# The store of each expert block's result moves from ScalarE's DMA queue to GpSimd's, behind a later gather

## The reference, cut to what matters

```python
def expert_block(args):
    e, tok, g = args
    xb = ht[tok]
    hid = jax.nn.silu(xb @ w1[e]) * (xb @ w3[e])
    return (hid @ w2[e]) * g[:, None].astype(ht.dtype)

yb = lax.map(expert_block, (blk_e, slot_tok.reshape(n_blocks, MOE_BLOCK), slot_gate.reshape(n_blocks, MOE_BLOCK)))
out = jnp.zeros_like(ht).at[slot_tok].add(yb.reshape(n_slots, -1))
```

## Time and profile before

| | us |
|---|---|
| median of 3 runs | 1793.36 |
| lowest and highest run | 1793.09, 1797.89 |
| span of the profiled execution | 1795.6 |
| PE busy in it | 1488.8 (83%) |
| DVE busy | 1117.0 (62%) |
| ACT busy | 684.6 (38%) |
| POOL busy | 239.6 (13%) |
| MoE blocks of layer 0, first gather to last store landed | 509.2 to 941.6 |
| MoE blocks of layer 1, first gather to last store issued | 1409.1 to 1758.5 |

### The profile page before, as it was taken

One profiled execution on the slowest core, in us unless ns is written; L12 is line 12 of the kernel. 1 busy time (PEld: TensorE's weight loads), 2 busy tenths in 40 slices (PEclk: granted clock), 3 DMA queues, 4 the chain that ended last, 5 costly groups with the idle time before them and its releaser, 6 DMA issues. The chain is left out here.

```text
span 1795.6 us, 21028 instructions
## 1 busy us (share of the span) xinstructions
PE 1488.8 (83%) x6626; PEld 1046.2 (58%) x6627; DVE 1117.0 (62%) x1421; ACT 684.6 (38%) x807; POOL 239.6 (13%) x172
## 2 busy tenths in 40 slices
PE   3889997579559999999972998999996499999981
PEld 2444554234248778778862444787743477777871
DVE  2289999853568764866517123655634688887744
ACT  3201010121137754755425002333311377777732
POOL 0000000000011110201102001555500010211201
PEclk9999998789769999999995997999998699999995
DMA  9465764020079977995828002000010799999964
GB/s 316 138 214 187 249 223 170 3 82 36 24 258 374 388 258 262 389 350 188 303 82 304 20 0 94 2 1 1 1 49 34 257 340 382 390 377 383 374 232 176
DMA packets 154127, 354.93 MB, mean 198 GB/s; under 512 B 6128, under 2 KB 23264, under 8 KB 154080
## 3 DMA queue, kind: packets, MB, share of 16 engines
q1 hardware_dynamic: 137552, 298.68, 45.5%
q0 software_dynamic: 8784, 31.99, 5.0%
q10 hardware_dynamic: 7744, 23.68, 3.3%
HBM read 318.57 MB, written 35.75 MB: 197 GB/s over the span
## 5 line engine op out<-in xcount | busy, mean ns | idle before, releaser
L1344 DVE TENSOR_TENSOR W_LO<-WRAW,W_HI 128x2048 fp32r<-128x2048 f32 x192 | 430.9, 2287 | 166.9 <-ACT W_HI L1268 166.8
L1268 ACT ACTIVATE W_HI<-WRAW 128x2048 fp32r<-128x2048 f32 x192 | 356.8, 1908 | 190.6 <-DMA WRAW<-in_moe_w 152.6
L1205 PE MATMUL PS<-W_HI,XLO 128*128 128x512 f32 x624 | 254.7, 408 | 34.7 <-DVE XLO L1353 34.7
L1207 PE MATMUL PS<-W_HI,XHI 128*128 128x512 f32 x624 | 249.0, 399 | 0.0
L1206 PE MATMUL PS<-W_LO,XHI 128*128 128x512 f32 x624 | 248.2, 398 | 0.0
L970 PE MATMUL PS<-HT,RING 128*128 128x512 f32 (+1 forms) x512 | 173.0, 494 | 6.8 <-DVEq L1041 6.8
L1205 PEld LDWEIGHTS PS<-W_HI,XLO 128*128 128x128 f32 x624 | 120.6, 193 | 67.4 <-issue 38.1
L970 PEld LDWEIGHTS PS<-HT,RING 128*128 128x128 f32 x512 | 96.5, 192 | 85.8 <-issue 72.4
L1744 POOL TENSOR_SCALAR HT<-HT,AR 128x512 f32<-128x512 f32 (+1 forms) x64 | 110.2, 1723 | 235.9 <-DVE AR L1699 235.6
L1207 PEld LDWEIGHTS PS<-W_HI,XHI 128*128 128x128 f32 x624 | 120.1, 192 | 26.4
L1205 PE MATMUL PS<-W_HI,HLO 128*128 128x512 f32 x312 | 126.5, 405 | 10.7 <-DVE HLO L1365 9.5
(11 more groups left out here) (220 smaller groups left out, 1971.6 us busy)
## 6 DMA issues: line engine op xcount, KB each, us to landing
WRAW<-in_moe_w SPq DMA_DIRECT2D x96, 2048.0 KB, 12.0
RING<-in_w_mod SPq DMA_DIRECT2D x24, 2048.0 KB, 14.3
moe_out<-YO ACTq DMA_DIRECT2D x39, 512.0 KB, 7.1
RING<-in_conv_pw SPq DMA_DIRECT2D x16, 512.0 KB, 5.3
moe_out<-NIL SPq DMA_DIRECT2D x15, 512.0 KB, 13.3
ROWS<-rows_of_layer SPq DMA_DIRECT2D x12, 512.0 KB, 5.9
RING<-in_attn_w_qkv SPq DMA_DIRECT2D x3, 2048.0 KB, 15.8
moe_in<-RING SPq DMA_DIRECT2D x10, 512.0 KB, 2.6
```

What stands on the lines that cost most here:

```text
L1205: pe.matmul(to, lo, W_HI[:, q, at:at + 512], start=start, stop=False)
L1207: return pe.matmul(to, hi, W_HI[:, q, at:at + 512], start=False, stop=stop)
L1268: nc.scalar.activation(part(W_HI, q, p), part(WRAW, q, p), ACT.Copy).then_inc((w2_hi if q == 2 else w_hi)[L], 1)
L1344: nc.vector.tensor_tensor(part(W_LO, q, p), part(WRAW, q, p), part(W_HI, q, p).bitcast(F32), ALU.subtract).then_inc(lo[L], 1)
```

## The change

ACT keeps the copy to `YO` but no longer issues the store. POOL issues it: after the gather of block b has been issued, POOL waits for `ya_ready` to reach b-1 (ACT's copy of block b-2), issues the store of block b-2, and goes on to wait for the gather of block b+1. The semaphore `y_out`, which counts stores landed, is no longer shared by the two layers but one for each. Nothing else changes: the same 39 stores of 512 KB are made.

```diff
-        y_out = both("y_out")
+        y_out = [sem(f"y_out{L}") for L in range(2)]
@@ gpsimd
-                    with pool.Fori(1, n + 1) as b:
+                    def gather_next(b):
                         pool.wait_ge(xg_in[L], b * 16)
                         pool.wait_ge(xg_turned[L], b)
                         pool.wait_ge(idx_ready[L], 1)
@@
                         gather()
+
+                    def y_store(count, rows):
+
+                        pool.wait_ge(ya_ready[L], count)
+                        pool.dma_start(yd[L][rows, :], YO[:, :]).then_inc(y_out[L], 16)
+
+                    gather_next(1)
+                    gather_next(2)
+                    y_store(1, slice(0, P))
+                    with pool.Fori(3, n + 1) as b:
+                        gather_next(b)
+                        y_store(b - 1, bass.ds(b * P - 2 * P, P))
+                    y_store(n, bass.ds(n * P - P, P))
                     pool.wait_ge(xg_in[L], n * 16 + 16)
@@ scalar
-                    def y_store(b, rows):
+                    def y_copy(b):
                         act.wait_ge(w2_used[L], b + 1)
                         if not first(b):
                             act.wait_ge(y_out[L], b * 16)
                         nc.scalar.activation(YO[:, :].rearrange("p (a n) -> p a n", a=2), PS[:, 5:7, :],
                                              ACT.Copy).then_inc(ya_ready[L], 1)
-                        act.wait_ge(ya_ready[L], b + 1)
-                        act.dma_start(yd[L][rows, :], YO[:, :]).then_inc(y_out[L], 16)
```

More of the change, by code:

```diff
@@ L1309, in _, with block_step @@
                     silu(0)
-                    def block_step(b, rows):
+                    def block_step(b):
                         before, load = load_of(act, b - 1), load_of(act, b)
@@ L1315, in block_step @@
                         split_new(b, before, load, 1)
-                        if rows is not None:
-                            y_store(b - 2, rows)
+                        if not (isinstance(b, int) and b == 1):
+                            y_copy(b - 2)
                             split_new(b - 1, load_of(act, b - 2), before, 2)
@@ L1322, in block_step @@
                         hid_hi(b - 1)
-                    block_step(1, None)
-                    block_step(2, slice(0, P))
+                    block_step(1)
+                    block_step(2)
                     with act.Fori(3, n) as b:
-                        block_step(b, bass.ds(b * P - 2 * P, P))
+                        block_step(b)
                     last = last_block(act)
-                    y_store(act.value_load(INFO[0:1, LAST_BUT_ONE:LAST_BUT_ONE + 1], min_val=least - 2, max_val=nb - 2),
-                            bass.ds(last * P - P, P))
+                    y_copy(act.value_load(INFO[0:1, LAST_BUT_ONE:LAST_BUT_ONE + 1], min_val=least - 2, max_val=nb - 2))
                     split_new(last, load_of(act, last - 1), load_of(act, last), 2)
                     hid_hi(last)
-                    y_store(last, bass.ds(last * P, P))
+                    y_copy(last)
                 @block.vector
```

## The result

| | kernel before | changed kernel |
|---|---|---|
| median (us) | 1795.62 (1793.09 to 1799.93, 4 runs) | 1816.90 (1813.57 to 1828.57, 4 runs) |
| ratio | 1 | 1.0116, 95% interval 1.0078 to 1.0154 |
| span of the profiled execution (us) | 1795.6 | 1811.4 |

The change makes the kernel slower by 1.2%, some 21 us; 1858 was predicted, +64.6. In a second, larger set of runs it stood at 1813.31 us, ratio 1.0076 (1.0051 to 1.01). Direction and mechanism were right, the size was not: it is a third of the forecast. The profiled executions lie 15.8 us apart.

The account below looks back on a forecast made before the run. PE was nearly full, the DMA engines too where weights are new; the change would make a closed loop through the late gather set the pace. Layer 0 +27.2, layer 1 +34.8, ends +2.6: +64.6, so 1858 us, range 1797 to 1905.

Parts of the forecast that it names:

- The heavy loop: Turn to turn where w3 of one block and w2 of the block before are new: 20.7 us before the clock.
- the store on POOL: POOL's issue of the store within the heavy loop: 1.6 us, between ends of 0.94 and 2.99.
- `icur` copy: POOL's copy between store and gather in the heavy loop: 0.6 us, between 0.18 and 2.22.
- landing: From the gather's start to its landing in a heavy step: 9.6 us, between 9.1 and 11.3.
- clock, mean per heavy step: PE's waits lower the granted clock in every second heavy step, at 1.9 us a drop: 0.9 us per heavy step.
- the ends: The end of each layer: last store lands 1.8 us later, ACT's relief gives -0.5; together +2.6 us for both layers.
- Light steps: Steps in which w3 of one block and w2 of the block before aren't both new: 18.1 us, between 17.7 and 18.8.
- ACT's relief: ACT loses 0.53 us of issue per block: worth nothing in the loop, -0.5 us before each layer's last `HHI`.
- the gather still lands in time: Rival, chance 0.18: with the lower ends the loops keep the pace of the kernel before, 1796 us.
- Faster: Rival, chance 0.06 for over 0.3%: ACT's relief brings w2 loads forward 0.5 us and removes PE's waits, at most to 1772.
- Much slower: Rival, chance 0.12: the gather's rows wait in POOL's queue behind the store's, 2.5 us in 35 steps, 1944 us.
- DMA share: Sign in heavy steps: the DMA engines' share falls to about 0.85 to 0.9 as PE waits.

Follow-up runs that it names:

- the first experiment: The changed kernel with each store still on POOL but moved one gather later, gather of block b before the store of block b-3: 1797.77 us, ratio 0.9987.
- the seventh experiment: The changed kernel, with ACT again waiting for its own `YO` copy before going on, though it issues no store: 1787.99 us, ratio 0.9941.
- the longer chain: The changed kernel with nine small POOL copies and a wait for them between the store and the next gather: 1984.19 us, ratio 1.1017.
- the sixth experiment: The changed kernel with the same wait for the `YO` copy, but behind it first the gather, then the store, both on POOL: 1804.51 us, ratio 1.003.

## Why the prediction was right, and where it wasn't

**The mechanism held.** Store soon after the `YO` copy, gather about 9 us behind the turn (10 was said), PE waiting for `XG` and no longer for `XLO`: as said. The heavy loop was put at 20.7 us and is 19.54 in the step above:

| term | predicted | measured |
|---|---|---|
| turn's end to the end of `YO` | 6.6 | 6.62 |
| to the store's start | 0.19 | 0.69 |
| the store on POOL | 1.6 | 0.56 |
| gap | 0.3 | 0 |
| `icur` copy | 0.6 | 0.21 |
| to the gather's start | 0.75 | 0.76 |
| landing | 9.6 | 9.6 |
| the turn | 1.04 | 1.10 |
| clock, mean per heavy step | 0.9 | about 0.1 |

**The step that failed** is the size of two terms of the heavy step, 21.6 us forecast and 19.6 measured: POOL's instructions between copy and gather, and the clock. First POOL. For the store, between 0.94 and 2.99, I took 1.6, and it takes 0.56, below both ends. The Trainium skill (SBUF — State Buffer, Who interferes with whom) says that DVE with two SBUF inputs holds up those instructions of GpSimd that read SBUF, and infers that descriptor writing, which needs the other interface, isn't held up by it. The trace agrees for the plain store: 0.57 us in the median of 39 stores, even inside a `W_LO` group (1623.91 in the first experiment). The `icur` copy was overrated by 0.4, for another reason: it falls between two groups of DVE (`W_LO` ends at 1529.17 and begins again at 1530.23). The gap of 0.3 isn't there. Together these three were 1.7 us too much; 0.5 us too little for the store's start leave 1.2 per heavy step. (Why POOL starts the store 0.69 us behind the copy, where ACT needed 0.19, isn't shown.) The clock, 0.9 forecast and 0.1 measured, makes the other 0.8.

**A right term by luck.** The landing, 9.6, was read from ten gathers of which seven are held up by DVE (2.24 to 3.08 us on POOL), and it came out right because the changed kernel holds up nearly every one (2.74). The seventh experiment has the same order of store and gather with a free gather, and that lands after 7.1 us. The prediction has no term for this.

**The clock.** I charged every second heavy step with 1.9 us. In the two loops of the changed kernel there are two drops, both in layer 1, of 3.4 us each. The first comes right behind a wait of PE, and the stretches are (columns as in the earlier trace rows):

```profile
1657.30:1659.30 2.00, 0.00 (x0) 0.00 (x0) 2.00 (x2) 0.00 (x0) 0.00 (x0) 1.00 1.04 412
1659.50:1662.90 3.40, 3.40 (x13) 3.01 (x13) 1.69 (x3) 1.69 (x2) 0.00 (x0) 0.50 1.03 416
```

The second also follows a wait, of 1.92 us; PE's other waits for `XG`, up to 2.3 us, were followed by none. A drop costs less here than in the earlier trace rows, too: the two steps are 20.57 and 20.85 us long against about 19.6, so 1.0 to 1.3, and PE's next wait is shorter for it (1.06 and 1.29). The kernel before has three drops in the same loop, the changed one two, so the change didn't add to them; I had charged for the new ones and taken none off. With waits of 5.5 us, in the longer chain, nearly each heavy step has one: so the charge exists, but this kernel seldom pays it.

**In sums.** The profiled span is 49 us short of the forecast. The heavy steps were 19.35 us (layer 0) and 19.59 (layer 1) in the mean, not 21.6: 9 x 2.25 + 14 x 2.0 = 48 us. Of the rest, the ends (6.1 less than forecast) are nearly undone by the 4.4 us elsewhere. Light steps were put at 18.1 and measured 18.18. Layer 0 came out at +7.9 instead of +27.2, layer 1 at +7.1 instead of +34.8.

**The ends.** I had +2.6 for both and found -3.5. From turn 22's end to the first gather of the combining stage it is 23.39 us against 24.44, in layer 1 21.38 against 23.90. The changed kernel's lines:

```profile
932.38 1.02 ACT L1313 ACTIVATE YO<-PS 128x1024 f32<-128x1024 f32 x1 [11.24 <-PE PS L1220]
933.88 0.60 ACT L1306 ACTIVATE HHI<-PS 128x512 fp32r<-128x512 f32 x1 [0.48 <-issue]
...
944.43 0.56 POOL L1194 DMA_DIRECT2D moe_out<-YO  x1 [9.77 <-ACT YO L1313]
...
950.19 0.99 POOL L1410 DMA_INDIRECT RING<-moe_out,DST  x1 [5.21 <-POOLq L1136]
```

`HHI` starts 0.48 us after the copy, not 2.62. So ACT is relieved of 2.1 us at this place, four times the 0.53 that I took: with the issue goes the wait for its own copy. The seventh experiment, which has the wait and not the issue, stands halfway, at 1.52 us. The last store lands 2.9 us after its issue on POOL, 2.6 on ACT: my +1.8 was nearly nothing. The remaining +4.4 us of the span lie in code that is the same in both; the stretch between the expert stages (turn 22 of layer 0 to turn 0 of layer 1) scatters from 496 to 509 us over the profiled executions, so they say nothing of the change.

**What I held to be worth nothing** decided most. I had written that ACT's relief lies beside PE's longer path. It does, but it also brings DVE's `W_LO` of w2 forward until it starts 0.39 us ahead of the gather. The seventh experiment takes this back and is 25 us faster. Of the rivals, "the gather still lands in time" was the nearest: a gather that isn't held up lands in 7 us, and then the late order costs PE only 0.5 us per step. "Faster" named a relief of ACT that helps; nothing shows one in the loop. "Much slower", a gather behind its store's bytes, isn't seen with the store ahead: the seventh experiment's gathers land after 7.1 us with a store some 1.9 us before them. With the store behind, in the sixth experiment, both are slow.

**DMA share** I expected to fall to 0.85 or 0.9 as PE waits. It stayed at 0.98, while ACT's waits for weights fell from 61.4 to 3.3 us. So in these kernels the share doesn't tell whether the DMA engines set the pace; what the engines waited for does.

## What to carry to other kernels

Ask of a moved instruction what runs beside it at the new place: here a late gather cost 1% or went with a gain of half of one, by whether a two-input DVE instruction started 0.4 us before it or 0.2 us after. A DMA share near 1 doesn't show that the DMA engines set the pace, and a rate over a stretch that moves fixed bytes is only its length: look for who waited for which transfer. Count the stretches at the half clock too; in the kernel before they were 5.1 us of layer 1's loop. Cutting the long DVE instructions in two was the cheapest cure (0.9932 and 0.996). Read a nearby instruction's price by what it touches (the gather reads indices, the plain store none), not as a middle between its neighbours.

## What the runs showed of the hardware

- A gather's issue on POOL takes 0.96 us alone. If it starts during a DVE subtraction of two SBUF tensors, it ends 0.9 us after that instruction does: 2.74 us beside 128x2048, 1.79 beside 128x1024. A gather that starts 0.18 us before DVE isn't held up (0.97). A plain store takes 0.57 in either place. Nine 128x1 copies take 5.34 us beside two such subtractions, and one takes 0.21 alone.
- Between kernels a held-up gather lands later, 9.7 us against 6.9 to 7.1 from its start, so by more than the 1.8 us that its issue takes longer. Within one kernel the difference is smaller (turns 3 to 14 of layer 1): 9.8 to 10.4 against 8.6 to 9.3 in the sixth experiment, 9.3 to 11.3 against 7.6 to 9.7 in the kernel before. So the hold-up isn't all that makes a landing late.
- At a DMA share of 0.98 to 1.01 the rate in layer 1 was 362 (gather 2.74 us on POOL), 368 (2.06), 371 (1.82), 379 (1.74), 384 (1.18), 385 (0.97) and 386 GB/s (0.96), for 97.7 to 98.9 MB each. Three kernels fall out of this row: 360 at 2.10, and 378 and 380 at 1.17 and 1.24. The loop's length was moved in two ways that share only this time: by cutting DVE's instructions, and by leaving them whole and letting the gather start first. How a slow issue would slow the other transfers was not tried, and there is at least one more cause.
- The granted clock falls to 0.50, the 1.2 GHz level, within or behind waits of PE, in stretches of 3.4 us in the changed kernel's loops (two) and the kernel before's (three), of 6.8 us and more in the longer chain. In layer 1's loop these were 10.2 us in the kernel before, 6.8 in the changed one, 13.7 in the sixth experiment, and none in the six kernels whose layer-1 loop takes less than 279 us.
